# Attention value products with the queries stationary, maxima one step sooner, one convolution tile summed by ScalarE and adding transfers

## What is computed

```python
def conformer_conv(u, dw_w, dw_b, ln_g, ln_b):
    a, gte = jnp.split(u, 2, axis=-1)
    v = a * jax.nn.sigmoid(gte)
    v = dwconv(v, dw_w, dw_b)                 # 31 taps, 512 channels, 512 tokens
    return jax.nn.silu(layer_norm(v, ln_g, ln_b))
def attend(q_nope, q_rope, k_nope, k_rope, v):
    s = (jnp.einsum('bqhd,bkhd->bhqk', q_nope, k_nope)
         + jnp.einsum('bqhr,bkr->bhqk', q_rope, k_rope)).astype(jnp.float32) * SOFTMAX_SCALE
    p = jax.nn.softmax(s, axis=-1).astype(v.dtype)
    return jnp.einsum('bhqk,bkhd->bqhd', p, v)         # v: 64 columns a head
def merge_groups(conv_out, attn_out, w_o, b_o):
    b, n = conv_out.shape[:2]
    cat = jnp.concatenate([conv_out, attn_out.reshape(b, n, N_HEADS * V_DIM)], axis=-1)
    return cat @ w_o + b_o
```

## Time and profile before

| | us |
|---|---|
| median of three runs | 1121.14 |
| lowest and highest | 1116.96, 1121.83 |
| the profiled execution, its own time | 1116.9 |
| its span | 1115.1 |
| outside the span | 1.8 |
| attention's loop (568.63 to 687.83 us of the span) | 119.20 |

### The profile page before, as it was taken

One profiled execution on the slowest core, in us unless ns is written; L12 is line 12 of the kernel. 1 busy time (PEld: TensorE's weight loads), 2 busy tenths in 40 slices (PEclk: granted clock), 3 DMA queues, 4 the chain that ended last, 5 costly groups with the idle time before them and its releaser, 6 DMA issues.

```text
span 1115.1 us, 14984 instructions
## 1 busy us (share of the span) xinstructions
PE 1089.3 (98%) x5935; PEld 886.7 (80%) x5935; DVE 793.1 (71%) x1290; ACT 557.0 (50%) x987; POOL 97.4 (9%) x123
## 2 busy tenths in 40 slices
PE   7999999999999999999999999999999999999997
PEld 4678888888888888888867666778888888888886
DVE  5877898878677746758897898876656565645427
ACT  6576566666234357754256665466444444432311
POOL 0222111112322000101000002000000000000001
PEclk9999999999999999999999999999999999999999
DMA  9742433345355743121110221123323232252201
GB/s 381 272 194 114 152 124 128 130 168 199 124 197 223 277 189 113 77 90 56 41 38 1 76 76 39 38 76 114 110 80 113 76 113 80 110 193 90 78 36 76
DMA packets 22368, 135.54 MB, mean 122 GB/s; under 512 B 2545, under 2 KB 2969, under 8 KB 8474
## 3 DMA queue, kind: packets, MB, share of 16 engines
q1 hardware_dynamic: 19936, 128.46, 31.2%
q10 hardware_dynamic: 2362, 6.12, 1.6%
HBM read 132.45 MB, written 2.12 MB: 121 GB/s over the span
## 4 chain that ended last, share of the span: by engine, by line
PE 79%; DVE 9%; ACT 5%; DMA 3%; issue 2%; POOL 1%; SPq 0%; DVEq 0%; ACTq 0%
PE PB L185 77%; DMA RAW<-in_wstream 3%; ACT WH L199 2%; DVE RAW L1452 2%; DVE WL L206 2%; PE PB L193 1%; POOL UPA L206 1%; DVE EARLY L1452 1%; DVE AT L234 1%; ACT HH L199 0%; DVE XL L214 0%; DVE UPA L214 0%; SPq L182 0%; ACT L200 0%; ACT DH L199 0%
## 5 line engine op out<-in xcount | busy, mean ns | idle before, releaser
L185 PE MATMUL PB<-HH,WH 128*128 128x512 f32 (+1 forms) x880 | 338.4, 385 | 4.1 <-DVE HL L206 1.9
L206 DVE TENSOR_TENSOR WL<-RAW,WH 128x1024 fp32r<-128x1024 f32 (+3 forms) x172 | 196.4, 1148 | 197.7 <-ACT WH L199 197.2
L185 PE MATMUL PB<-HH,WL 128*128 128x512 f32 (+1 forms) x880 | 332.8, 378 | 0.0
L185 PE MATMUL PB<-HL,WH 128*128 128x512 f32 (+1 forms) x880 | 331.4, 378 | 0.0
L199 ACT ACTIVATE WH<-RAW 128x1024 fp32r<-128x1024 f32 (+3 forms) x172 | 166.6, 975 | 265.3 <-PE PB L185 234.0
L185 PEld LDWEIGHTS PB<-HH,WH 128*128 128x128 f32 x880 | 165.6, 188 | 37.7 <-issue 2.4
L185 PEld LDWEIGHTS PB<-HH,WL 128*128 128x128 f32 x880 | 165.5, 188 | 31.2
L185 PEld LDWEIGHTS PB<-HL,WH 128*128 128x128 f32 x880 | 165.7, 188 | 30.0 <-issue 0.5
L214 DVE SCALAR_TENSOR_TENSOR CV<-VP,PC,CV 128x512 f32<-128x512 f32 x120 | 88.0, 776 | 0.7
L185 PE MATMUL PB<-WL,AH 128*128 128x512 f32 (+1 forms) x198 | 72.4, 366 | 0.0
L185 PE MATMUL PB<-WH,AH 128*128 128x512 f32 (+1 forms) x198 | 72.4, 366 | 0.0
(11 more groups left out here) (300 smaller groups left out, 1710.3 us busy)
## 6 DMA issues: line engine op xcount, KB each, us to landing
RAW<-in_wstream SPq DMA_DIRECT2D x101, 1024.0 KB, 4.9
EARLY<-in_wstream SPq DMA_DIRECT2D x7, 1024.0 KB, 13.8
RAW<-in_wstream SPq DMA_DIRECT2D x5, 768.0 KB, 4.3
RAW<-in_wstream SPq DMA_DIRECT2D x5, 512.0 KB, 3.5
XL<-in_x SPq DMA_DIRECT2D x2, 1024.0 KB, 6.5
HB<-in_x SPq DMA_DIRECT2D x2, 1024.0 KB, 6.3
out<-XL SPq DMA_DIRECT2D x8, 256.0 KB, 2.0
ROWS<-in_rows ACTq DMA_DIRECT2D x3, 512.0 KB, 7.9
```

Source lines behind the costliest of these rows:

```text
L185: return self.put(lambda e: e.matmul(o, l, r, start=start, stop=stop, skip_group_check=skip))
L206: return self.put(lambda e: e.tensor_tensor(o, a, b, op))
```

## The change

1. **Value products.** In each head the products are now made twice, three key tiles at a time: `values(h, 0)` after the scores of t = 3, `values(h - 1, 1)` after the scores of (h, 0). The powers are now the stationary operand, in tiles of 64 queries whose results go by turns to PSUM partitions 0 to 63 and 64 to 127, and 65 columns of VG move (64 values and a one). The result is queries x values. PR has five buffers instead of three.
2. **Divisors.** VectorE takes the reciprocals of 4 columns straight from PSUM (`divisors(h)`), and ScalarE copies the head out with four scaled activations of 128x64 (`values_out`). Ln and Exp of the sums, and the product with the divisors, are gone. TensorE turns each finished pair back with four transposes (`turned_pair`), and the high and low parts are taken from PSUM.
3. **Maxima.** `maxima(h + 1, j)` moves from step t = j + 1 to t = j on TensorE, VectorE and ScalarE.
4. **Convolution.** Tile 1 leaves VectorE (93 taps in `conv_plan` instead of 124, with other counts in `conv_step`). ScalarE makes each tap's product (`tap_product(k)`, 128x512) and GpSimd adds it into CV[1] with an accumulating transfer of 256 KB, SBUF to SBUF, each issued when the one before has landed.

```diff
-        return 5 if h == 7 else (3, 2, 5 if h < 6 else 2, 0, 1, 4)[t] if h % 2 == 0 else (0, 0, 3, 0, 1, 2)[t]
+        return (2, 1, 2, 2, 2, 1)[t] if h == 7 else (0, 0, 5, 0, 0, 2)[t] if h % 2 == 0 else (0, 0, 3, 0, 0, 1)[t]
+
+    ADDED = 1
+
+    def added_at(h, t):
+
+        if h == 7:
+            return 27 + t if t < 4 else None
+        return 6 + 3 * h + t // 2 if t % 2 == 0 else None
...
+        for k in range(1, 31):
+            g.wait_ge(S_.a_cv, ("prod", k))
+            if k == 1:
+                g.wait_ge(S_.a_cv, ("prod", 0))
+            else:
+                g.wait_ge(S_.added, ("tap", k - 1))
+            x = added_to(k)
+            g.put(lambda e: e.dma_start(CV[:, ADDED, :], x, accum_op=ADD)).then_inc(S_.added, ("tap", k), by=16)
+
         g.wait_ge(S_.p_sm, ("s", 7, 0))
         for j in (1, 2):
-            g.wait_ge(S_.v_cv, ("cv", j))
+            convolved(g, j)
...
+        def tap_product(k):
+
+            x, w = VP[:, ADDED, k:k + S], col("conv_dw_w_2", 4 * k + ADDED)
...
+            if k < 3:
+                a.wait_ge(S_.p_sm, "rqd" if k == 2 else ("rkd", 1))
+            elif k in (6, 7, 8):
+                a.wait_ge(S_.p_blk, 85)
+                a.wait_ge(S_.added, ("tap", 5))
+            else:
+                a.wait_ge(S_.added, ("tap", k - 2 if k < 6 else k - 3))
+            a.act(added_to(k), x, ACTF.Identity, scale=w).then_inc(S_.a_cv, ("prod", k))
...
-            if s > 2:
-                a.wait_ge(S_.p_sm, ("o", (s - 3) // 6, (s - 3) % 6))
-            a.act(PR[s % 3], main.of(("s", h, t)), ACTF.Exp, scale=SCALE).then_inc(S_.a_ev, ("s", h, t))
+            if s > 4:
+                a.wait_ge(S_.p_sm, ("o", (s - 5) // 6, (s - 5) % 6 // 3))
+            a.act(PR[s % 5], main.of(("s", h, t)), ACTF.Exp, scale=SCALE).then_inc(S_.a_ev, ("s", h, t))
...
-            a.copy(OTS[i][me[0]:me[1], :], z[me[0]:me[1], :])
-            a.copy(SU[i][me[0]:me[1], :], z[other[0]:other[1], :]).then_inc(S_.a_ax, ("ov", h))
...
+            for i in range(4):
+                c = 65 * i + h % 2
+                op = a.act(o[:, 128 * i + 64 * (h % 2):128 * i + 64 * (h % 2) + 64], z[:, c:c + 64], ACTF.Identity,
+                           scale=RCP[:, 4 * (h % 2) + i:4 * (h % 2) + i + 1])
+            op.then_inc(S_.a_ax, ("ov", h))
...
-                if 1 <= t <= 4 and h < 7:
-                    maxima(h + 1, t - 1)
-                if t == 5 and h in (2, 4):
+                if t < 4 and h < 7:
+                    maxima(h + 1, t)
+                if t == 4 and h in (2, 4, 6):
                     pair_high(h // 2 - 1)
...
+                if added_at(h, t):
+                    tap_product(added_at(h, t))
+        values_out(7)
...
-        divisors(2, 3, between=last_squares)
-        pair_high(2)
+        last_squares()
         pair_high(3)
...
-            c = 192 * (h // 2) + 64 * (h % 2)
-            pe.mm(bk, VG[:, t, c:c + 128], PR[(6 * h + t) % 3], t == 0, t == 5).then_inc(S_.p_sm, ("o", h, t))
+            c = 192 * (h // 2) + 127 * (h % 2)
+            for t in range(3 * part, 3 * part + 3):
+                pe.wait_ge(S_.a_ev, ("s", h, t))
+                p = PR[(6 * h + t) % 5]
+                for i in range(4):
+                    for n in range(2):
+                        q = 128 * i + 64 * n
+                        op = pe.mm(bk[64 * n:64 * n + 64, 65 * i:65 * i + 65], p[:, q:q + 64], VG[:, t, c:c + 65],
+                                   t == 0 and i == 0, t == 5 and i == 3, True)
+            op.then_inc(S_.p_sm, ("o", h, part))
+
+        def turned_pair(p):
...
+            for i in range(4):
+                op = pe.tr(bk[:, js(i)], OTS[p % 2][:, js(i)], IDN[:, :])
+            op.then_inc(S_.p_sm, ("ot", p))
...
-                if t:
-                    values(h, t - 1)
-                elif h:
-                    values(h - 1, 5)
-                if 1 <= t <= 4 and h < 7:
-                    maxima(h + 1, t - 1)
+                if t == 3:
+                    if h in (2, 4, 6):
+                        turned_pair(h // 2 - 1)
+                    values(h, 0)
+                elif t == 0 and h:
+                    values(h - 1, 1)
+                if t < 4 and h < 7:
+                    maxima(h + 1, t)
...
-            rows(ys, B_O + n, merged(k), n == 0, n == 3, (2, 3) if n == 1 else range(4))
+            if n == 0:
+                rows(ys, B_O + n, merged(k), True, False, (0, 1), False)
+                turned_pair(3)
+            rows(ys, B_O + n, merged(k), n == 0, n == 3, (2, 3) if n < 2 else range(4))
             if n == 0:
                 conv_sums()
```

More of the change, by code:

```diff
@@ L590, in conv_step, with added_to, convolved @@
     def conv_step(h, t):
-        return 5 if h == 7 else (3, 2, 5 if h < 6 else 2, 0, 1, 4)[t] if h % 2 == 0 else (0, 0, 3, 0, 1, 2)[t]
+        return (2, 1, 2, 2, 2, 1)[t] if h == 7 else (0, 0, 5, 0, 0, 2)[t] if h % 2 == 0 else (0, 0, 3, 0, 0, 1)[t]
[4 more added lines that the diff above has]
+        return 6 + 3 * h + t // 2 if t % 2 == 0 else None
+    def added_to(k):
+        return (DG[:, :], OT[:, :])[k % 2] if k < 6 else (ROWS5[:, 3584:4096], ROWS5[:, 7680:8192], DG[:, :])[k % 3]
+    def convolved(eng, j):
+        if j == ADDED:
+            eng.wait_ge(S_.added, ("tap", 30))
+        else:
+            eng.wait_ge(S_.v_cv, ("cv", j))
     def conv_plan():
-        plan, ends, left, last = {}, {}, {0: 0}, None
+        plan, ends, left, last = {}, {ADDED: "end"}, {0: 0}, None
         places = [(p, n) for p, n in CONV_AT.items()] + [((h, t), conv_step(h, t)) for h in range(8) for t in range(6)]
-        for p, n in places + [("end", 124)]:
+        for p, n in places + [("end", 93)]:
             for j, at in GLU_AT.items():
-                if p == at:
+                if p == at and j != ADDED:
                     left[j] = 0
@@ L1211, in act_prog @@
             a.copy(CH[:, m, :], CQ[:, m, :]).then_inc(S_.a_h, ("cq", m))
+        tap_product(0)
+        tap_product(1)
         split(86)
         split(87)
+        tap_product(2)
         glu(2, 82)
+        tap_product(3)
         split(88)
         split(89)
+        tap_product(4)
         glu(3, 84)
+        tap_product(5)
         def key_high(h):
@@ L1982, in dve_prog @@
                     query_low(h + 2)
[L1983 to L1984 removed]
+                if t == 5 and h in (2, 4, 6):
+                    pair_low(h // 2 - 1)
                 if t == 5 and h == 2:
@@ L1990, in dve_prog @@
         cm, cv_, cr, cq_ = (CNT[:, 4 * i:4 * i + 4] for i in range(4))
+        divisors(7)
         conv("end")
         split(B_O + NW)
-        for p in (2, 3):
-            pair(p)
         st = aux.of("cvs")
@@ L2002, in dve_prog @@
         v.tt(cv_, cv_, cq_, SUB).then_inc(S_.v_s, "nv")
-        for p in (2, 3):
-            pair_low(p)
+        pair_low(3)
         v.wait_ge(S_.g_s, "npw")
```

73 lines of the change are left out of this document (37 added, 36 removed).

## The result

The changed kernel takes 1136.01 us (median of 4 runs, 1133.64 to 1139.14) beside 1120.64 us (median of 4) for the kernel before. The ratio is 1.0147, with a 95% interval of 1.0120 to 1.0174 (the two medians alone give 1.0137). It is 1.5% slower. The forecast was 1125.5 us in a range of 1115 to 1133, so the measured time lies above the whole range.

A forecast was written before the change was run, and what follows sets the result against it. TensorE, busy for 98% of the span, was taken as the bound. Loop -4.5, transposes +0.5, wait before the sums +7.9 and clock +0.5 gave +4.4 us: 1125.5 us against a median of 1121.1, range 1115 to 1133.

The forecast's parts named there:

- Value products: TensorE in attention's loop: 48 products of 0.85 us go (-40.9), 16 groups of 1.84 us come (+29.4).
- Maxima: TensorE in the loop waits for VectorE's reductions, 0.39 us twice a head in seven heads: +5.5 us.
- A power waits behind at most one product: ScalarE in the loop: its added products stay hidden by TensorE, and five PR buffers cover a power's wait.
- The chain: GpSimd's adding transfers end late, so TensorE stands 7.9 us before the convolution's sums, which start at 697.6.
- up to L near 5 the chain keeps up: In heads 0 to 6, three taps in about 15 us, so the chain falls behind only at the end.
- L: Time from a tap's finished product to the landing of its adding transfer, taken as 3.6 us.
- Rival D: Chain falls behind within the loop, L over 5, ScalarE waits with powers behind: 1150 us or more; chance 0.07.
- Hidden already, worth nothing: VectorE in the loop loses some 30 taps at 0.69 us each; priced at nothing.
- The clock: The gap before the convolution's sums may lengthen the lower clock there: 0 to 1.7 us, taken as 0.5.
- The small tiles: A clock below 1.00 in the loop, from small tiles using less of the array, would show the forecast wrong.
- The forecast loop: Attention's loop falls from 119.2 to 114.7 us and ends near 683.3 instead of 687.83: -4.5 us.
- GpSimd's quicker additions: After tap 30 lands, GpSimd's four additions with two semaphores were taken as 6.3 us before the sums.

The follow-up runs named there:

- x6: The changed kernel with the transfer chain ended at tap 20 and VectorE making taps 21 to 30 of tile 1: 1122.5 us, 1.0036 to the kernel before.
- x13: x5 with ScalarE's last diagonal ahead of the power of t = 4 again: 1118.89 us, 1.0006 to the kernel before.
- x5: x6 with the next head's maxima spaced by long work and ScalarE's last diagonal behind the power of t = 4: 1115.2 us, 0.9963 to the kernel before.
- x12: The changed kernel with ScalarE's two 512 KB row transfers issued later, behind the last `pair_high(3)`: 1135.94 us, 1.0156 to the kernel before.
- x3: The changed kernel with GpSimd clearing one column in place of each adding transfer, all waits and products kept: 1119.58 us, 1.0009 to the kernel before.
- x2: The kernel before with only the convolution part added (ScalarE's products and adding transfers for tile 1): 1136.1 us, 1.0156 to the kernel before.
- x1: The changed kernel with the convolution back on VectorE, all 124 taps in their old places: 1133.31 us, 1.0133 to the kernel before.
- x10: x5 without any transfer, all 124 taps on VectorE and spread evenly: 1128.95 us, 1.0091 to the kernel before.
- x4: x1 with the maxima back at steps t = 1 to 4: 1126.59 us, 1.0075 to the kernel before.

## Why the prediction was wrong, step by step

**Value products: right.** 1.84 us a group were forecast and 1.74 measured, and the records are 0.032 us apart. The 16 groups are 1.6 us cheaper together than the sum had it. The row of the recurrence's own form, taken over a form that pays at each key tile, was the right one. What a visit to the small tiles costs at its two ends came out as 0.19 us, not 0.34.

**Maxima: the mechanism right, the size a little low.** A cycle is 1.67 us as worked out. TensorE loses about 6.8 us by them in the loop, against 5.5; the rest is mostly in odd heads, where a short wait follows maxima 2 as well. That the place makes the cost is shown by x6 and x13: with a long piece between them 0.30% comes back, about 3.4 us. It isn't all gone: x5's trace still has 3.2 us of waits for reductions.

**"A power waits behind at most one product": this step failed.** It counted the products that the change adds to ScalarE and not the diagonals that it moves. The last diagonal now stands ahead of the power of t = 4 and waits for a reduction. The five PR buffers don't help: in the row of x13 it is a score product that waits, for a PSUM bank (`take`) that the power has not read yet. That costs 3.0 us in three heads of the loop. x13 puts the diagonal back by itself, and 0.43% goes, about 4.8 us; its trace has two such waits, 2.2 us, and its loop is 3.6 us longer than x5's, so the rest of it isn't accounted for.

**The chain: the price of a tap right, "up to L near 5 the chain keeps up" wrong. This is the step that made the forecast fail.** L was forecast as 3.6 and is 3.82 undisturbed. But the forecast took one L for every tap, and so let tap 26 be issued at 673.3, on the ground that the chain keeps up before head 7. It was issued at 681.09. Tap 23 had taken 8.33 us beside a load of 1 MB (it lands in 6.1 itself), well over 5, and from then on the chain was behind. The next taps took 3.82, 4.43, 3.83, 4.83 and 3.80, and tap 29 took 7.72 beside the row transfers. The 4.43 and 4.83 are longer with no other data transfer beside them. In each of the two stretches the trace has one small transfer of instructions (0.02 and 0.01 MB), in x12's 3.95 and 4.03 too, and in none of the stretches of 3.8. That hints at a cause, but no run tests it. Added up, the last landing was 13.4 us later than forecast: 7.8 by the late issue of tap 26 and 5.6 in the five taps from it on. An estimate splits it another way. Product 26 was done at 676.96 and not at 673.3, 3.7 us late, as the loop was late; from there five taps of 3.82 would have ended at 696.1, 1.1 more by the price of a tap; the remaining 8.6 are disturbed taps.

x3, x6 and x2 show that it is this chain that costs: 1.4% of ratio with or without its transfers, 1.1% when it is cut at tap 20, 1.6% when it is put alone into the kernel before. That the load and the row transfers make taps 23 and 29 long is shown for 29 by x12. For 23 it rests on its place beside the load; no run moves the load.

**Rival D, which had 0.07, came in for one head.** Its mechanism, ScalarE waiting in `tap_product(k)` with powers behind, cost 1.33 and 3.03 us at the end of head 7. It was tied to L over 5 all through the loop; a chain of 3.8 with a few disturbed taps was enough.

**"Hidden already, worth nothing": this step failed for VectorE.** It was true of the kernel before, where 107.20 of 119.20 us were busy and TensorE full. It stops being true once reductions and reciprocals are asked for sooner and TensorE has less of its own to do meanwhile. x3 against x1 puts 13.7 us on the 31 taps and the places of the others, with the maxima where the changed kernel has them. The forecast used this relief without pricing it: its 5.5 us for the maxima count on little being queued on VectorE. In the traces of x1 and x10 TensorE waits for reductions behind taps, and all three kernels with all taps on VectorE and the new products (x1, x4 and x10) are slower than before. It doesn't explain the loss, but it explains what the experiments gain: x5 needs this relief.

**The clock: too small.** 0.5 us were forecast. The sums alone lost 3.3 by running at 0.50, TensorE having stood for 10.17 us ahead of them. A long gap isn't needed for a part of this: with 0.75 us of waiting ahead the sums take 5.4 us in x3, with 1.00 they take 5.4 in x6 and 4.5 in x5, the first products at full speed and the last at half. With no wait they took 3.5 in the kernel before. The small tiles, which the forecast had as a possible sign of trouble, didn't lower the clock: x5's loop ran at 1.00. And the first nine products of the projection are 0.42 apart instead of 0.23 (from 693.03 to 693.45), which is about 1.7 us more, after TensorE had stood for 3.03 of the 4.80 us up to 689.70:

```profile
684.90:689.70 4.80, 1.80 (x20) 1.22 (x20) 0.92 (x2) 1.17 (x3) 0.87 (x1) 1.00 0.32 56
689.70:693.50 3.80, 3.00 (x35) 2.69 (x36) 0.91 (x3) 1.97 (x7) 0.87 (x1) 0.50 0.40 69
```

The second row is the one with clock 0.50. The 1.7 us before the sums cost nothing themselves, since they lie ahead of a wait for GpSimd that ends when it ends; of the slow value group in that stretch about 0.8 is in the loop's length. The same holds for everything that made the loop longer. TensorE stood before the sums anyway, so a longer loop counts only as far as it made products of the chain late.

**The sum again, with what was measured.** The forecast loop, from 569.23, was 115.0 long (-4.5 against 119.5) and came out as 123.2. The 8.2 between are +1.3 for maxima, +3.0 for powers behind diagonals, +4.4 for powers behind the chain, +0.8 of clock and -1.6 for the groups, 7.9; 0.3 is left. The sums start 13.1 later than forecast, by the landing of tap 30 (13.4) less GpSimd's quicker additions. With +3.3 for the sums less the 0.5 that stood for it, +4.4 becomes +20.3, and 20.1 is there. Most of the terms are read from the one trace after, so their agreement is no independent test; the runs without transfers and with a shorter chain are.

## What to carry to other kernels

A chain of transfers that each wait for the landing before has no slack to make up a disturbed one: take its rate from a tap beside the largest transfer in the stretch, and end it well before its result is needed (cut at two thirds, together with the spaced maxima and the later diagonal, it turned 1.5% slower into 0.4% faster than before). When an instruction is moved on an in-order queue, list what now stands behind its wait, on every engine that issues a part of it. And time that was hidden before an edit has to be counted again after it: once one engine's work shrinks, relief of the next is no longer worth nothing.

## What the runs showed of the hardware

An adding transfer from one place of the core's memory to another, 256 KB, issued by GpSimd, took 3.82 us from issue to issue when chained, of which 0.87 is the issue itself; the plain copy took 2.82, with 0.55 of issue. Half the bytes, added, still took 3.2.

Beside a load of 1 MB an adding transfer took 8.33 us, and beside two of 512 KB 7.72 (7.83 in x2, and 3.86 in x12 without them), both about twice its own time, though the DMA share of the stretches was 0.62 and 0.73 (0.40 in 689.70 to 693.50, with tap 28 alone):

```profile
664.50:672.80 8.30, 8.04 (x119) 6.34 (x116) 5.63 (x9) 5.28 (x14) 0.87 (x1) 1.00 0.62 160
...
693.50:701.20 7.70, 7.02 (x27) 5.36 (x25) 4.42 (x6) 0.20 (x1) 0.87 (x1) 0.80 0.73 172
```

The products with ones, 128x1, stayed at the lower of TensorE's two levels for the whole of the sums (clock 0.50 in 710.70 to 717.50) though TensorE was busy in all of it, and took 6.8 us in x2 and x12 too, behind waits of 11.95 and 8.97 us; before, entering them from full work, they ran at 1.00.
